# Projecting the scan's result before its norm is known: a hybrid decoder trunk on one Trainium2 core

## The reference, cut to what matters

```python
y = ssd_chunked_scan(xs, dt, a, bmat, cmat) + d_skip[:, None] * xs
y = rms_norm(y * silu(z), norm_w)      # over 2048 features; norm_w is one factor per feature
mix = y @ w_out                        # 2048 x 1024
x = x + g1 * mix                       # g1: one factor per output feature
hf = rms_norm(x, gain) * (1 + sc2) + sh2
x = x + g2 * moe_swiglu(hf, ...)
```

## Time and profile before

| | us |
|---|---|
| median of three runs | 1634.1 |
| the profiled execution | 1636.98 |
| its span in the trace | 1634.8 |
| PE busy | 1593.6 (97%) |
| DVE busy | 1376.4 (84%) |
| ACT busy | 1105.1 (68%) |

### The profile page before, as it was taken

How to read it: one execution, slowest core, us unless ns; L and a number is a source line. 1 busy time by engine, 2 the same in 40 slices (tenths; PEclk the granted TensorE clock), 3 DMA queues, 4 the chain that set the end, 5 groups by cost and what they waited for, 6 DMA issues and landing times.

```text
span 1634.8 us, 24265 instructions
## 1 busy us (share of the span) xinstructions
PE 1593.6 (97%) x7455; PEld 1268.0 (78%) x7455; DVE 1376.4 (84%) x1560; ACT 1105.1 (68%) x1335; POOL 31.1 (2%) x31
## 2 busy tenths in 40 slices
PE   7989999999999989999999999999999999999998
PEld 2736888787778768788888888888888888888876
DVE  3667888886577897899899899899899899999997
ACT  2665544444465663787887887887877878878875
POOL 0000000000000000010000000000000000000300
PEclk9989999999999999999999999999999999999999
DMA  9776898884647415699999998999999999999994
GB/s 363 289 285 237 322 359 294 306 287 155 208 145 182 168 45 162 229 401 407 372 405 337 407 402 321 408 410 342 407 391 347 410 384 347 407 382 353 411 392 169
DMA packets 155258, 516.85 MB, mean 316 GB/s; under 512 B 18643, under 2 KB 21004, under 8 KB 155032
## 3 DMA queue, kind: packets, MB, share of 16 engines
q1 hardware_dynamic: 151304, 501.63, 82.4%
q0 software_dynamic: 3856, 14.16, 2.3%
HBM read 507.84 MB, written 12.09 MB: 318 GB/s over the span
## 4 chain that ended last, share of the span: by engine, by line
PE 87%; DVE 7%; ACT 3%; issue 2%; DMA 1%; SPq 0%; DVEq 0%; ACTq 0%
PE acc L2008 25%; PE acc L2015 25%; PE acc L2009 25%; DVE w_lo L1140 3%; PE xb L2392 2%; PE acc L2163 1%; DMA raw<-in_ada_w 1%; PE xb L2065 1%; PE acc L2518 1%; DVE cv L1695 1%; PE acc L1991 1%; PE acc L2497 0%; PE xb L2424 0%; ACT w_hi L695 0%; PE xb L2077 0%
## 5 line engine op out<-in xcount | busy, mean ns | idle before, releaser
L1140 DVE TENSOR_TENSOR w_lo<-raw,w_hi 128x1024 fp32r<-128x1024 f32 x832 | 989.9, 1224 | 131.4 <-ACT w_hi L695 102.7
L695 ACT ACTIVATE w_hi<-raw 128x1024 fp32r<-128x1024 f32 x832 | 865.0, 1059 | 261.7 <-PE acc L2015 234.2
L2008 PE MATMUL acc<-w_hi,g_hi 128*128 128x512 f32 x896 | 352.8, 394 | 0.0
L2009 PE MATMUL acc<-w_hi,g_lo 128*128 128x512 f32 x896 | 349.1, 390 | 0.0
L2015 PE MATMUL acc<-w_lo,g_hi 128*128 128x512 f32 x896 | 276.3, 390 | 0.2 <-DVE w_lo L1140 0.2
L2015 PEld LDWEIGHTS acc<-w_lo,g_hi 128*128 128x128 f32 x896 | 168.1, 188 | 36.3 <-DVE w_lo L1140 0.6
L2009 PEld LDWEIGHTS acc<-w_hi,g_lo 128*128 128x128 f32 x896 | 168.3, 188 | 33.8
L2008 PEld LDWEIGHTS acc<-w_hi,g_hi 128*128 128x128 f32 x896 | 168.3, 188 | 33.8
L2008 PE MATMUL acc<-w_hi,a_hi 128*128 128x512 f32 x448 | 179.1, 400 | 1.2 <-ACT xbc L990 0.5
L2009 PE MATMUL acc<-w_hi,a_lo 128*128 128x512 f32 x448 | 175.5, 392 | 0.0
L2008 PE MATMUL acc<-w_hi,e_hi 128*128 128x512 f32 x432 | 172.1, 398 | 0.0
(11 more groups left out here) (326 smaller groups left out, 1418.4 us busy)
## 6 DMA issues: line engine op xcount, KB each, us to landing
raw<-in_moe_w_gu SPq DMA_DIRECT2D x448, 512.0 KB, 8.1
raw<-in_moe_w_down SPq DMA_DIRECT2D x224, 512.0 KB, 5.4
raw<-in_ada_w SPq DMA_DIRECT2D x96, 512.0 KB, 6.5
raw<-in_ffn_w_gu SPq DMA_DIRECT2D x56, 512.0 KB, 5.5
raw<-in_ssm_w_in SPq DMA_DIRECT2D x40, 512.0 KB, 4.5
raw<-in_ffn_w_down SPq DMA_DIRECT2D x28, 512.0 KB, 4.8
raw<-in_ssm_w_out SPq DMA_DIRECT2D x16, 512.0 KB, 13.6
raw<-in_attn_w_qkv SPq DMA_DIRECT2D x12, 512.0 KB, 12.7
```

What stands on the lines that cost most here:

```text
L695: act.activation(w_hi[:, w % SPLIT, :], raw[:, no % RAW, :], ACT.Copy).then_inc(hi_ready, 1)
L1140: dve.tensor_tensor(w_lo[:, w % SPLIT, :], raw[:, no % RAW, :], r32(w_hi[:, w % SPLIT, :]), ALU.subtract).then_inc(raw_used, 1)
L2008: pe.matmul(o, l_hi[:, k, rows_], hi[:, col:col + HALF], start=new, stop=False)
L2009: pe.matmul(o, l_lo[:, k, rows_], hi[:, col:col + HALF], start=False, stop=False)
```

## The change

- The residual is no longer put into the accumulators, and y is no longer scaled ahead of the projection. The column factors norm_w are loaded as 16 rows of 128 (`y_rows`), turned by one more transpose in `dt_turn` and copied to `y_gain`; `gate_tile` multiplies a tile of `w_out` by g1 and by its column of `y_gain` in one instruction. The 1 MB broadcast load of norm_w goes, and its wait on SP.
- The row factor r_t is worked out during `wout` (from DVE's step 6 on) and applied behind it: `scaled_rows` writes x = acc * r_t + x, one instruction of 128x1024 per token block, and norm 3 then reads x like norm 2. The copies L775 go. PE issues two idle matmuls more at the start of norm 3 (`WARM_ROWS`).
- Seven tiles are gated ahead of the scan in place of eight, and the parts of the first four `wout` tiles are made ahead of or in the scan: `w_lo` 0 to 2 before unit 0, `w_lo` 3 after unit 0.
- Piece q = 0 of y is turned in two halves, by token: block 0 after unit 3, block 1 after unit 7. PE runs the first three tiles for token block 0 before it ends the last unit, the fourth behind it, and then the first four tiles for token block 1.
- `xd`, `xde` and `state` lie elsewhere, so that `y_hi` can be written during the scan.

```diff
-    GATED_AHEAD = 8
+    GATED_AHEAD = 7
+    BY_TOKEN = 4
@@ DVE, ahead of and in the scan
             for i in range(GATED_AHEAD):
                 gate_tile("wout", i)
+            early_lo("wout", 0, 3)
             unit_mid(0)
...
                 if u < 7:
                     unit_mid(u + 1)
+                if u == 4:
+                    y_turned(0, 0)
                 unit_out(u)
+                if u == 6:
+                    y_turned(0, 1)
                 if u < 6:
                     unit_in(u + 2)
+                if u == 0:
+                    early_lo("wout", 3)
-            dve.wait_ge(yss_ready, 8)
-            own(dve.reduce_sum(ss[:, :], yss[:, :, :], axis=AX.X))
...
-            y_scaled(0)
-            early_lo("wout", 0, 1)
-            y_turned(0)
...
@@ gate_tile
+                    dve.scalar_tensor_tensor(tile, tile, y_gain[:, i:i + 1], mod[:, MOD_SLOT[1][2], :], ALU.mult, ALU.mult).then_inc(gated, 1)
@@ dt_sum
+                own(dve.tensor_copy(y_gain[:, :], xb[c % 2][:, T * SH:T * SH + DI // P]))
                 dve.sem_inc(xb_done[c % 2], 1)
                 dve.sem_inc(dtv_ready, 1)
@@ scaled_rows, ahead of norm 3 on DVE
+                if t == 0:
+                    dve.wait_ge(rows_full, 3)
+                else:
+                    dve.wait_ge(w_used, spl0["norm3"])
+                own(dve.scalar_tensor_tensor(x[:, t, :], acc[m % 3][:, :], rs[:, t:t + 1], x[:, t, :], ALU.mult, ALU.add))
@@ ACT, in the scan
             for u in range(1, 8):
                 unit_decays(u)
+                if u == 1:
+                    early_hi("wout", 3)
+                if u == 5:
+                    y_turned(0, 0)
                 state_out(u - 1)
                 if u >= 2:
                     y_square(u - 2)
-            early_hi("wout")
+            y_turned(0, 1)
+            y_square(6)
             warm(ACT.Sqrt)
@@ norm 3 on DVE now has norm 2's order
+                    else:
+                        scaled_rows(0)
+                        scaled_rows(1)
+                        mean(0)
                     root(0)
@@ PE
+            def token_tile(stage, i, parts, lhs, t):
...
+                if i == 0:
+                    open_pair(n % 3, n // 3)
+                pe.wait_ge(hi_ready, w + 1)
+                for k, to, col in parts:
+                    o = acc[n % 3][:, to:to + HALF]
+                    pe.matmul(o, l_hi[:, k, rows_], w_hi[:, w % SPLIT, col:col + HALF], start=i == 0, stop=False)
+                    pe.matmul(o, l_lo[:, k, rows_], w_hi[:, w % SPLIT, col:col + HALF], start=False, stop=False)
+                pe.wait_ge(raw_used, lo_count(raw0[stage] + i))
...
+                if t == T - 1:
+                    mm.then_inc(w_used, 1)
...
+            def wout_tile(i, t):
+                token_tile("wout", i, wide(i), (y_hi, y_lo), t)
...
+            for u in range(7):
                 unit_out(u)
                 if u < 6:
                     unit_in(u + 2)
+                if u == 3:
+                    y_turn(0, 0)
+            y_stands(0, 0)
+            for i in range(3):
+                wout_tile(i, 0)
+            unit_out(7)
+            y_turn(0, 1)
+            wout_tile(3, 0)
             for t in range(T):
-                open_with_rows("wout", t)
-            y_turn(0)
-            y_stands(0)
+                y_turn(1, t)
+            y_stands(0, 1)
+            for i in range(BY_TOKEN):
+                wout_tile(i, 1)
+            for t in range(T):
+                y_stands(1, t)
             gemm("wout", [[wide(k) for k in range(2 * KD)]], (y_hi, y_lo), wout_steps)
```

More of the change, by code:

```diff
@@ L197, in build @@
     yss = place("yss", [P, T, SG], f32, F_AT + 3712)
+    y_gain = place("y_gain", [P, DI // P], f32, F_AT + 3776)
+    y_rows = place("y_rows", [DI // P, P], f32, F_AT + 2176)
     y_hi = place("y_hi", [P, DI // P, SEQ], f32r, A_AT)
@@ L1068, in _, with wout_steps @@
                     y_square(u - 2)
-            early_hi("wout")
+            y_turned(0, 1)
+            y_square(6)
             warm(ACT.Sqrt)
[L1071 to L1083, removed]
-            y_turned(0)
-            gemm("wout", None, (2 * KD,), lambda i: y_turned(i // 4 + 1) if i % 4 == 3 and i < 12 else None)
+            def wout_steps(i):
+                if i % 4 == 3 and i < 12:
+                    for t in range(T):
+                        y_turned(i // 4 + 1, t)
+                if i == 5:
+                    y_square(7)
+                    act.wait_ge(ld_router, 16)
+                    act.activation(w_r_hi[:, :, :], w_r[:, :, :], ACT.Copy).then_inc(small_hi, 1)
+                if i == 9:
+                    act.wait_ge(yms_ready, 1)
+                    act.activation(rs[:, :], ms[:, :], ACT.Sqrt).then_inc(yroot, 1)
+            gemm("wout", None, (2 * KD,), wout_steps)
             norm(3, "norm3")
@@ L1767, in unit_out, with y_turned @@
                 dve.tensor_tensor(y, y, z_s[:, c, 512 * g:512 * (g + 1)], ALU.mult).then_inc(y_ready, 1)
+            def y_turned(q, t):
+                part = (slice(None), slice(4 * q, 4 * q + 4), slice(t * P, (t + 1) * P))
+                piece_lo(y_piece(q, t), (y_hi[part], y_lo[part]))
             unit_in(0)
@@ L1787, in _ @@
-            own(dve.reciprocal(rs[:, :], rs[:, :]))
-            dve.wait_ge(ld_norm, 16)
-            def y_scaled(q):
-                for t in range(T):
-                    cols = slice(q * HALF, (q + 1) * HALF)
-                    dve.scalar_tensor_tensor(xbc[:, t, cols], xbc[:, t, cols], rs[:, t:t + 1],
-                                             mod[:, q // 2, (q % 2) * HALF:(q % 2 + 1) * HALF], ALU.mult, ALU.mult).then_inc(yn_ready, 1)
-            def y_turned(q):
-                for t in range(T):
-                    part = (slice(None), slice(4 * q, 4 * q + 4), slice(t * P, (t + 1) * P))
-                    piece_lo(pc0["ynorm"] + T * q + t, (y_hi[part], y_lo[part]))
@@ L1816, in wout_steps @@
                 if i % 4 == 3 and i < 12:
-                    y_turned(i // 4 + 1)
+                    for t in range(T):
+                        y_turned(i // 4 + 1, t)
+                if GATED_AHEAD <= i + 3 < 2 * KD and i > 3:
+                    gate_tile("wout", i + 3)
+                if i == 6:
+                    dve.wait_ge(yss_ready, 8)
+                    own(dve.reduce_sum(ss[:, :], yss[:, :, :], axis=AX.X))
+                    dve.tensor_scalar(ms[:, :], ss[:, :], 1.0 / DI, EPS, ALU.mult, ALU.add).then_inc(yms_ready, 1)
@@ L2030, in open_with_rows @@
                     pe.matmul(o[:, cols], ident, x[:, t, cols], start=True, stop=False)
+            def token_tile(stage, i, parts, lhs, t):
+                l_hi, l_lo = lhs
+                n, w = pr0[stage] + t, spl0[stage] + i
+                rows_ = slice(t * P, (t + 1) * P)
+                if i == 0:
[6 more added lines that the diff above has]
+                pe.wait_ge(raw_used, lo_count(raw0[stage] + i))
+                for k, to, col in parts:
+                    o = acc[n % 3][:, to:to + HALF]
+                    mm = pe.matmul(o, l_hi[:, k, rows_], w_lo[:, w % SPLIT, col:col + HALF], start=False, stop=False)
+                if t == T - 1:
+                    mm.then_inc(w_used, 1)
             def gemm(stage, groups, lhs, after=None, rows_of=None):
@@ L2039, in gemm @@
                     for n, parts in enumerate(tiles):
+                        if stage == "wout" and i < BY_TOKEN:
+                            i += 1
+                            continue
                         if rows_of and i == KD // 2:
```

138 lines of the change are left out of this document (71 added, 67 removed).

## The result

The changed kernel takes 1622.4 us (median of 4 runs, 1621.4 to 1623.1), the kernel before 1633.8 (4 runs, 1633.0 to 1637.2). The ratio is 0.9926, with a 95% interval of 0.9912 to 0.9940: 12.1 us less, interval 9.8 to 14.4. Forecast were 1623.7 and the range 1620.0 to 1628.8.

The account below looks back on a forecast made before the run. Ahead of the experts' stage, the series scan, norm factor, scaling, turning, parts was taken as the bound, with PE idling. Terms -12.5 + 1.8 + 0.3 = -10.4 us gave 1623.7 us; range 1621.5 to 1626.5, 8 in 10 for 1620.0 to 1628.8.

Parts of the forecast that it names:

- The middle: Unit 6's outputs to tile 4 on PE: 28.00 us become 15.0, less 0.5 for the scan, so 12.5 us earlier.
- the two places named: `y_lo` of piece 1 and `w_lo` 4, ready at 603.5 and 604.6; PE needs them at 604.95 and 605.85.
- The scan: `y_lo` (0,0) has no cover on DVE during the scan, so unit 6's outputs on PE end 0.5 us later.
- The norm: From `wout`'s last matmul to the logits' second half: 1.4 to 2.4 us longer, taken as 1.8.
- The start: `y_gain`'s copy ahead of the signal ACT waits for costs 0.3 us on the path (0 to 0.4).
- VectorE was not the bound: Rival: DVE becomes the bound of the scan's end, 5.7 us more, 1629.4; chance 0.10.
- The clock did not turn against the change: Rival: PE stays at half clock through the new dense stretch, 15.0 us more, 1638.7; chance 0.03.
- the clock help further on: Rival: full clock from 662 to 675 us and in the norm, 1.8 + 0.4 better, 1621.5; chance 0.09.
- the early-tiles rival: Tiles 0 to 2 run behind unit 7 after all; 3.1 us idle and the clock's 1.7 return, 1628.5; chance 0.08.

Follow-up runs that it names:

- experiment 6: Changed kernel with two or four token tiles ahead of unit 7, not three, or the lone `y_lo` behind unit 7 on VectorE: ratio 0.9940 each.
- experiments 1 to 3: Kernel before with three idle matmuls ahead of unit 7 (1.0018); without the residual on PE (1.0010); with PE kept busy from unit 6 to first tile (0.9990).
- experiment 7: Changed kernel with the copy into `y_gain` behind the signal that ACT's softplus waits for: ratio 0.9921 to the kernel before.
- Experiments 1 and 4: Kernel before with three idle matmuls ahead of unit 7: ratio 1.0018; changed kernel without tiles by token: ratio 0.9993 to the kernel before.
- experiment 5: Changed kernel without tiles by token, with idle matmuls for both waits (three ahead of unit 7, two ahead of first tile): ratio 0.9976 to the kernel before.

## Why the prediction was right

**The middle (-12.5, with the scan's +0.5 in it).** Measured -12.56 from the scan's start to E. The eight token tiles, unit 7 and the turns took 600.64 - 585.69 = 14.95 us, against 15.0. The step that carried it was to count on PE's timeline what the new order holds and to ask for each piece whether VectorE has it ready. Each of those answers held: gates at 1.28 (both bounds, 1.22 and 1.49, were further off), no delay of the scan's start, the 1.27 us wait (1.35 said) hidden. The reserve behind it was given as 1.2 to 1.5 us; at the two places named that holds, but in experiment 6 four tiles ahead added 1.37 to the wait and PE then waited 1.06, so it was 0.3 at the tightest place. That place was not on my list: the turn of piece 1, which waits for `y_lo` (0,1) to free its buffer.

**The scan (+0.5).** Measured +0.66: `y_lo` (0,0) has no cover, as said.

**The norm (+1.8).** Measured +1.52, inside 1.4 to 2.4. But this difference flatters it: in the profiled execution before, the clock was down at this place, and the same code took 8.93 us in experiments 1 to 3, not 9.56. Against that it is +2.15, a third of a microsecond over the term, and the sum of the stages would be -10.15 and not -10.78, with the -10.4 said between the two. The scaled half came at E + 2.41 and not E + 2.05, because the second update of x waits 0.24 for the end of the first and the mean waits 0.24 again; the turn came at E + 3.62 against E + 3.7, since PE's idle matmuls set it. The rest was at full clock, the lower end of the 11.0 to 11.9 said.

**The start (+0.3).** Measured +0.29; moving the copy (experiment 7) takes 0.34 off, so the copy was all of it.

**The rivals.** VectorE was not the bound. The clock did not turn against the change: 1.00 over the 14.50 us of dense work. The Trainium skill, "TensorE: Matmul & The Clock Gate", section "What's actually happening", has the throttled level as the default that activity releases; the dense stretch agrees. Nor did the clock help further on: ahead of the experts it was 0.85 over 11.5 us, where before it was 0.87 over 13 us, 1.7 us of cost in both (the rival's sum has 1.8 for this 1.7). Experiments 1 and 4 add what the forecast did not use: behind waits of 3.26 and 3.08 us the slow stretch went to whatever stood there, so its price depended on whether that work was covered. I had put the clock's price in the early-tiles rival at 1.7; without those tiles it was 2.4 to 3.8. That rival, 1628.5, was also too mild for the whole of them: a median of 1631.2 without any tile by token, beside 1633.2 for the kernel before.

**What the forecast left unsaid.** Unscaling y alone, which is the change's first half, gives hardly a measurable gain (0.9993): it takes 4.18 us off up to E, less than it might since the bound moves from the norm's chain to PE at half clock behind its wait, and the costs of the start, the scan and norm 3 take 2.5 back. The second half takes 9.04 us off up to E and adds nothing to those costs, so it is what shows in the time.

## What to carry to other kernels

When a chain is shortened, ask at once what the engine behind it did in its shadow: PE's slow clock cost 0.46 us while a norm covered it and at least 2.4 once the norm was gone. Fill a wait with work of the next stage rather than with idle matmuls. If idle matmuls must do, fill every wait up to the first work that nothing covers: filling only the first of two moved the slow stretch onto the output tiles here. And see that they stand ahead of the wait in the engine's list; behind it they are plain delay (1.42 us in experiment 5). Where one engine's queue has a wait with little behind it to spare, one more tile ahead of it can cost nearly its whole length (1.25 of 1.37 us), so try the neighbours of such a count.

## What the runs showed of the hardware that I had not expected

- Removing a slow stretch moved it: with three idle matmuls the granted clock was 1.00 up to the end of the 3.26 us wait, then 0.76 and 0.50 for 8.3 us over the turn and first tiles, and the kernel got 2.9 us slower.
- The same rows behind the same 1.25 us wait ran at full clock in one execution and at half in another (0.66 and 1.11 for four transposes).
- Two 128x1024 updates of different rows of x, with nothing else between them, stood 1.52 us apart at 1.28 each, 0.24 of it idle. In this kernel VectorE waits for each update's own end before it goes on (`own`). The gates, which also take 1.28 each but have no such wait, stand 1.20 apart.
